# A hybrid decoder step on one core: weights streamed by half chunks, biases within the parts, and 21 dots moved between tiles

## The chip, the core and the metric

The kernel runs on one core of one Trainium2 chip, in one launch, all in float32. A core has five engines, each with an instruction queue of its own: PE (TensorE, matmul), DVE (VectorE), ACT (ScalarE), POOL (GpSimd) and SP (SyncE, which here issues loads and stores); 16 DMA engines serve them all. The engines meet at semaphores. The metric is the device time of one launch in microseconds (us), lower is better. TensorE's clock has two levels, 1.2 and 2.4 GHz; the profile shows the share that was granted.

## The reference, cut to what matters

512 prompt tokens and 8 x 4 sample tokens go through one layer of width 1024.

```python
mod = silu(c) @ ada_w + ada_b                 # 12 pieces of 512 columns, one row per sequence
sh1, sc1, gt1, sh2, sc2, gt2 = split(mod, 6)
h = rmsnorm(x, g_mix) * (1 + sc1) + sh1
z = h @ w_in                                  # 1024 x 3336
hm = mlstm(q, k, v, gates, C, n, m)           # 4 heads of 128, matrix memory C
oa = swa(sq, sk, sv, sinks, window=128)       # 4 heads, 2 of keys and values
yc = cb * short_conv(cc * ch, conv_w)
x = x + gt1 * (concat(hm, oa, yc) @ w_out)
h = rmsnorm(x, g_ffn) * (1 + sc2) + sh2
q = h @ wq                                    # 8 heads, two half keys each
idx, g = top 16 of the sums of the two top 16 # of 128 x 128 experts
act = gelu(einsum('thkd,td->thk', u_tab[idx], h))
x = x + gt2 * einsum('thk,thkd->td', g * act, v_tab[idx])
y = rmsnorm(x, final_g)
```

Each token needs 128 rows of `u_tab` (a dot product each) and 128 rows of `v_tab` (a weighted sum), 4 KB a row.

## The kernel before, in words

**Two parts.** The mixer comes first, up to a barrier at about 681 us; then the experts' part, which gathers rows of the two tables and works on them.

**The mixer's tiles.** The prompt is four tiles of 128 tokens, the sample is one tile of 32. Ahead of tile 0 stands a first stage that makes four of the twelve modulation rows; the tails of tiles 0 and 1 make the other eight. A modulation row takes three steps on PE: `ada_part` (L1344) multiplies the eight 128-row pieces of a chunk of `ada_w` in four column groups of 32, ACT copies the part, and `ada_row` (L1351, L1352) or, for one row spread over 128 partitions, `ada_rows` (L1358, L1359) folds the four groups with one matmul and adds the bias with a second one, the pick. DVE copies the row (L1231) and SP stores it (L961). A tile goes through its seven chunks of `w_in` (`chunk`, L615; 392, 512, 512, 512, 384, 512 and 512 columns in the order gates, q, k, v, sv|cb, cc|ch, o), with the mLSTM, the attention and the convolution between them, then `w_out` (L696) and the residual (L888 to L892). The first four transposed pieces of the normed rows are copied by ACT, the others by DVE (L791, hT).

**The stream.** SP loads the chunks of `ada_w`, `w_in` and pieces of `peer_wq` in a fixed order through a ring of three slots of 2 MB (`w_stream`, class `Stream`, load at L257). Chunk k waits until chunk k-3 is used up; a `wq` piece of 1 MB takes a slot too. PE waits for a whole chunk (`landed`).

**The first tile's experts, ahead of time.** From tile 1 on the mixer also routes tile 0's tokens. From tile 2 on GpSimd gathers their 128 rows of `u_tab` per token (L346), one row for each of 128 tokens at a time, into a ring of eight buffers in `low_rows`; DVE takes the dot product with the tile's rows (L333) and so frees the buffer. Where the dots stand is a table, `DOTS_IN`: gaps B to J, R, A and Z of each tile's code on DVE, C to Z of the sample's. The rows lie in SBUF for tiles 2 and 3; for the sample DVE copies them to PSUM three times (`row_to`, L339).

**The sample's tile.** It also loads the key and value caches and, last, the state C (2 MB into the stream's slots, L1543); PE transposes C in eight steps (L1734), and DVE and ACT copy the odd and even ones out (L1650, L1593). DVE makes Km, keys masked by sequence (L1670), for PE's update of C (L1762 to L1776; DVE's L1690 adds it up).

**The seam.** After the barrier GpSimd makes five constants (L1917 to L1924), then begins to gather `v_tab` rows (L1946); SP loads what the experts need, `subkeys` among it, which PE transposes first (L2442).

Of the kernel before, what the change touches and what calls it, by code (L numbers as in the profile page):

```python
# [106 lines left out]
class ConstantBuffers:  # L107

    def __init__(self, nc, ctx, space):  # L110
# [5 lines left out]
        self.pool_ready = sem("const_pool")  # L116
# [32 lines left out]
def constants_pool(nc, pool, K, C):  # L149
# [52 lines left out]
    fill(K["bias"][:, :, :], [[0, AH], [-1, 2 * P]], ALU.is_ge, NEG, P, 1).then_inc(C.pool_ready, 1)  # L202

class Stream:

    def __init__(self, X, s, s2):
# [18 lines left out]
        self.adas = [c for kind, c in self.order if kind == "ada"]  # L227

    def where(self, kind, i):
        k = self.order.index((kind, i))  # L230
        return k, k % RING

    def landed(self, pe, kind, i):

        k, slot = self.where(kind, i)
        pe.wait_ge(self.X.stream_in[slot], 16 * (k // RING + 1))
        return slot
# [12 lines left out]
    def load(self, sp, I, kind, i):  # L250

        k, slot = self.where(kind, i)
        if k >= RING:
            self.consumed(sp, k - RING)
        a, b = (i * 512, i * 512 + 512) if kind == "ada" else (i * 256, i * 256 + 256) if kind == "wq" else CHUNKS[i]
        src = I["ada_w" if kind == "ada" else "peer_wq" if kind == "wq" else "w_in"][0].rearrange("(kc p) n -> p kc n", p=P)
        sp.dma_start(self.X.wr[:, slot, :, 0:b - a], src[:, :, a:b]).then_inc(self.X.stream_in[slot], 16)  # L257

class Modulation:  # L260

    def __init__(self, space):
# [6 lines left out]
        self.pick_all = space.take(12, 4 * P, "p (c r) -> p c r", r=P)  # L270
# [6 lines left out]
DOTS_IN = {(2, "C"): 3, (2, "D"): 2, (2, "E"): 8, (2, "F"): 4, (2, "H"): 3, (2, "I"): 2, (2, "J"): 6, (2, "R"): 2, (2, "A"): 3,  # L277
# [9 lines left out]
AHEAD_SIGNALS = ("a_sub_in a_rows_in a_sq a_sq_ready a_h_ready piece_full piece_out keys_done a_routed a_used a_step").split()  # L287

class Ahead:  # L290
# [64 lines left out]
    def act_squares(self, act):  # L355
# [7 lines left out]
    def norm(self, dve, chain):
# [4 lines left out]
        dve.wait_ge(s["a_sq_ready"], 1)  # L368
# [4 lines left out]
    def pe_point(self, pe, t, w, e):  # L373
# [107 lines left out]
class Mixer:  # L481

    def __init__(self, nc, ctx):
# [3 lines left out]
        def ps(name, shape):  # L488
# [3 lines left out]
        self.stream_in = [nc.alloc_semaphore(f"mix_stream_in{i}") for i in range(RING)]  # L492
# [60 lines left out]
ADA_SIGNALS = ("ada_c_in c_sgm c_silu ct_ps ct_ready picks bias_in gain_in part_full part_out row_full row_ready row_out0 row_out1 "  # L553
               "rows_full").split()

class Tile:
# [49 lines left out]
    def chunk(self, pe, i):  # L607
# [5 lines left out]
        slot = X.stream.landed(pe, self.kind, i)  # L613
        for kc in range(KC):
# [171 lines left out]
    def dve_front(self, dve, chain, K, behind_rows=None):  # L786
# [44 lines left out]
        if self.kind == "sample":  # L831
            dve.wait_ge(s["m_in"], 16)
# [1707 lines left out]
```

## Time and profile before

| | us |
|---|---|
| median of 3 runs | 1984.42 (1981.6 to 1985.84) |
| the profiled execution | 1981.32 |
| its span | 1979.5 |
| PE busy | 1577.7 (80%) |
| DVE busy | 1212.3 (61%) |
| POOL busy | 1096.7 (55%) |
| ACT busy | 466.6 (24%) |

Busy shares are means over stretches that differ: in the experts' part the DMA engines are always busy, in the mixer the engine that ends a stretch last changes. So the busy times are read by stretch, and the waits at the end of each. In a row of a timeline the first number is the start, the second the duration of the group; `[2.88 <-DMA ...]` is the idle time just before it and what ended it.

### The profile page before, as it was taken

How to read it: one execution, taken by the hardware profiler on the slowest of the kernel's cores; microseconds unless marked ns; L12 is line 12 of the kernel's file. 1: busy time of each engine (PE TensorE's matmuls, PEld its weight loads, DVE VectorE, ACT ScalarE, POOL GpSimd, SP SyncE). 2: the span in 40 equal slices, each digit the busy share in tenths (PEclk: the TensorE clock that was granted, in tenths of full speed). 3: DMA queues.
4: the chain of work that ended last, by engine and by line, in shares of the span. 5: the costliest groups of instructions: out<-in, count | busy, mean ns of one | idle time of the engine just before them, and what ended most of it. 6: DMA issues, size and time to landing. Idle time of an engine off the chain costs nothing.

```text
span 1979.5 us, 17753 instructions
## 1 busy us (share of the span) xinstructions
PE 1577.7 (80%) x5461; PEld 734.4 (37%) x5461; DVE 1212.3 (61%) x3132; ACT 466.6 (24%) x1212; POOL 1096.7 (55%) x1168
## 2 busy tenths in 40 slices
PE   6989987788767568768888888888888788899933
PEld 1534544545236113223333343333433344344400
DVE  2223266886866602116767776877667679889973
ACT  1131311312102121212222222231222222323321
POOL 3000033443342245777777777777767677677774
PEclk8989998988875689998999999999999899999966
DMA  9696669798896599999999999999999999999996
GB/s 330 239 365 215 225 232 363 262 355 311 248 393 211 188 413 385 411 405 389 408 419 420 420 419 419 419 419 420 419 402 420 393 412 416 391 414 417 417 353 259
DMA packets 237565, 713.42 MB, mean 360 GB/s; under 512 B 23102, under 2 KB 49056, under 8 KB 237457
## 3 DMA queue, kind: packets, MB, share of 16 engines
q0 software_dynamic: 156672, 570.49, 72.8%
q1 hardware_dynamic: 80488, 140.73, 20.1%
q10 hardware_dynamic: 312, 1.07, 0.2%
q8 instruction: 45, 0.74, 0.1%
q14 instruction: 48, 0.39, 0.0%
HBM read 704.42 MB, written 8.25 MB: 360 GB/s over the span
## 4 chain that ended last, share of the span: by engine, by line
DMA 20%; PE 16%; POOL 13%; DVE 10%; issue 5%; ACT 2%; POOLq 0%; ACTq 0%; DVEq 0%
DMA v_rows<-in_peer_v_dram,expert_idx_ring 12%; PE ps_y L2373 9%; POOL u_rows L1932 6%; DMA v_rows<-in_peer_v_dram,tile_idx 5%; DVE u_rows L2152 5%; POOL v_rows L1938 5%; PE ps_r L2347 4%; POOL v_rows L1946 2%; DMA u_rows<-in_peer_u_dram,expert_idx_ring 2%; PE ps_y L2401 2%; ACT wt_diag L2043 1%; DVE key_scores_w L2163 0%; DVE top_i L2165 0%; DMA v_rows<-in_peer_v_dram,sample_idx 0%; DVE top L2164 0%
## 5 line engine op out<-in xcount | busy, mean ns | idle before, releaser
L2373 PE MATMUL ps_y<-v_rows,wt_diag 128*128 128x512 f32 x1536 | 731.6, 609 | 135.4 <-DMA v_rows<-in_peer_v_dram,expert_idx_ring 111.3
L2152 DVE CUSTOM_DVE_ANT_0 u_rows<-u_rows,ps_y 128x1024 f32<-128x1024 f32 x360 | 422.8, 1218 | 109.4 <-DMA u_rows<-in_peer_u_dram,expert_idx_ring 108.5
L2373 PEld LDWEIGHTS ps_y<-v_rows,wt_diag 128*128 128x128 f32 x1536 | 272.8, 191 | 533.9 <-issue 475.2
L1932 POOL DMA_INDIRECT u_rows<-in_peer_u_dram,expert_idx_ring x384 | 366.2, 954 | 137.4 <-issue 100.9
L1938 POOL DMA_INDIRECT v_rows<-in_peer_v_dram,expert_idx_ring x384 | 365.5, 952 | 118.7 <-issue 98.9
L615 PE MATMUL ps_z<-w_stream,hT 128*128 128x512 f32 (+5 forms) x560 | 252.1, 609 | 45.6 <-DMA w_stream<-in_w_in_dram 24.4
L346 POOL DMA_INDIRECT low_rows<-in_peer_u_dram,tile_idx x128 | 140.2, 1095 | 232.0 <-DVE tile_dots L333 169.2
L2401 PE MATMUL ps_y<-v_rows,wt_diag 64*64 64x512 f32 x1024 | 134.2, 643 | 58.5 <-DMA v_rows<-in_peer_v_dram,tile_idx 52.0
L615 PEld LDWEIGHTS ps_z<-w_stream,hT 128*128 128x128 f32 (+1 forms) x560 | 103.3, 189 | 173.4 <-issue 139.0
L1946 POOL DMA_INDIRECT v_rows<-in_peer_v_dram,tile_idx x128 | 123.4, 964 | 72.2 <-PE ps_y L2401 45.2
L2162 DVE MAX8 top<-key_scores 128x8 f32<-128x128 f32 x64 | 18.2, 285 | 172.2 <-ACT key_scores L2023 172.2
L2347 PE MATMUL ps_r<-wq,hT_next 128*128 128x256 f32 x512 | 116.9, 382 | 5.0 <-ACT hT_next L2013 5.0
L2043 ACT ACTIVATE wt_diag<-ident,wts 128x128 f32<-128x128 f32 x384 | 117.4, 388 | 14.2 <-DVE wts L2158 14.2
L2039 ACT ACTIVATE act_val<-dots 128x8 f32<-128x8 f32 x48 | 10.0, 209 | 456.1 <-DVE dots L2152 456.1
L2347 PEld LDWEIGHTS ps_r<-wq,hT_next 128*128 128x128 f32 x512 | 97.3, 191 | 32.9 <-issue 15.7
L899 POOL TENSOR_TENSOR z_cc_ch<-z_cc_ch 128x256 f32<-128x256 f32 (+1 forms) x5 | 3.6, 727 | 186.3 <-DVE z_cc_ch L840 186.3
L2401 PEld LDWEIGHTS ps_y<-v_rows,wt_diag 64*64 64x64 f32 x1024 | 39.6, 139 | 147.4 <-issue 117.2
L2152 DVE CUSTOM_DVE_ANT_0 u_rows<-u_rows,h_cur 128x1024 f32<-128x1024 f32 x24 | 28.9, 1233 | 91.1 <-DMA u_rows<-in_peer_u_dram,expert_idx_ring 91.1
L333 DVE CUSTOM_DVE_ANT_0 low_rows<-low_rows,tile_rows 128x1024 f32<-128x1024 f32 x63 | 75.6, 1250 | 7.1 <-DMA low_rows<-in_peer_u_dram,tile_idx 7.1
L696 PE MATMUL ps_z<-w_out,qT_kT 128*128 128x512 f32 (+1 forms) x160 | 74.0, 622 | 4.7 <-DVE low_rows L1231 4.7
L333 DVE CUSTOM_DVE_ANT_0 low_rows<-low_rows,ps_n 128x1024 f32<-128x1024 f32 x47 | 56.0, 1216 | 12.6 <-DMA low_rows<-in_peer_u_dram,tile_idx 12.2
L2386 PE MATMUL ps_y<-v_rows,wt_diag 128*32 128x512 f32 x96 | 21.4, 1039 | 46.9 <-DMA v_rows<-in_peer_v_dram,sample_idx 46.9
(444 smaller groups left out, 1722.0 us busy)
## 6 DMA issues: line engine op xcount, KB each, us to landing
w_stream<-in_w_in_dram SPq DMA_DIRECT2D x25, 2048.0 KB, 13.0
w_stream<-in_ada_w_dram SPq DMA_DIRECT2D x12, 2048.0 KB, 12.9
w_stream<-in_peer_wq_dram SPq DMA_DIRECT2D x8, 1024.0 KB, 9.5
wq<-in_peer_wq_dram SPq DMA_DIRECT2D x4, 2048.0 KB, 42.5
w_stream<-in_w_in_dram SPq DMA_DIRECT2D x5, 1568.0 KB, 8.5
w_stream<-in_w_in_dram SPq DMA_DIRECT2D x5, 1536.0 KB, 16.2
u_rows<-in_peer_u_dram,expert_idx_ring POOLq DMA_INDIRECT x384, 10.5
v_rows<-in_peer_v_dram,expert_idx_ring POOLq DMA_INDIRECT x384, 10.8
```

Source lines behind the costliest of these rows:

```text
L333: self.nc.vector.tensor_tensor_reduce(self.rows[:, k % NB, :], self.rows[:, k % NB, :], self.row, 1.0, 0.0, ALU.mult, ALU.add, self.keep[" ...
L346: self.nc.gpsimd.indirect_dma_start(self.rows[:, k % NB, :], None, U, bass.IndirectOffsetOnAxis(self.keep["idx0"][:, k:k + 1], 0)).then_in ...
L615: mm = self.nc.tensor.matmul(X.ps_z[i % 2][0:n, 0:b - a], X.hT[:, kc, 0:n], X.wr[:, slot, kc, 0:b - a], start=(kc == 0), stop=(kc == KC - 1))
L696: mm = nc.tensor.matmul(X.ps_z[c][0:n, :], X.mixT[:, kc, 0:n], X.w_out[:, kc, c * 512:(c + 1) * 512], start=(i == 0), stop=(i == KC - 1))
L1932: g.indirect_dma_start(u_rows[:, j, :], None, U, bass.IndirectOffsetOnAxis(where[:, j:j + 1], 0))\
L1938: g.indirect_dma_start(v_rows[:, j, :], None, V, bass.IndirectOffsetOnAxis(where[:, j:j + 1], 0))\
L1946: g.indirect_dma_start(v_rows[:, j, :], None, V, bass.IndirectOffsetOnAxis(idx0[:, k:k + 1], 0))\
L2043: a(diag[:, par, j, :], K["ident"][:, :], ACT.Copy, scale=wts[:, par, j:j + 1])\
L2152: v.tensor_tensor_reduce(u_rows[:, j, :], u_rows[:, j, :], row[:, :], 1.0, 0.0, ALU.mult, ALU.add, dots[:, par, j:j + 1]).then_inc(s["u_us ...
L2347: mm = nc.tensor.matmul(ps_r[:, 0, 0:256], hT[:, kc, :], wq[:, kc, bass.ds(h * 256, 256)], start=(kc == 0), stop=(kc == KC - 1))
L2373: mm = nc.tensor.matmul(ps_y[:, c * 512:(c + 1) * 512], diag[:, par, j, :], v_rows[:, j, c * 512:(c + 1) * 512], start=(first and j == 0), ...
L2401: mm = nc.tensor.matmul(ps_q[b * HP:(b + 1) * HP, half, c * 512:(c + 1) * 512], diag[rows, i % 2, j + b, 0:HP], v_rows[rows, j + b, c * 51 ...
```

## The change

It has five parts. **Halves:** the ring has six half slots of 1 MB. A chunk of `ada_w` or `w_in` comes as two loads of four 128-row pieces each, with a semaphore for each half slot; PE begins when the first half is there, and a half's slot is loaded again when that half is used (`half_used`, or the chunk's own signal for the second). A `wq` piece takes one half slot. **Bias:** `ada_part` adds the bias with one pick in its first half, and the picks behind the folds are gone, `pick_all` with them. **Constants:** GpSimd makes the experts' five constants at the start of the mixer. **Dots:** 21 of the 128 move from the sample's gaps to those of tiles 2 (5) and 3 (16); the prompt tiles had 66 and now have 87, the sample 62 and now 41. **Sample:** ACT makes the three row copies, all eight copies of C's transposes and Km. A number of semaphores are merged.

```diff
 class Stream:
...
-    def consumed(self, sp, k):
-        kind, i = self.order[k]
-        if kind == "ada":
+        kind, i, half = self.parts[k]
+        if kind == "wq":
+            sp.wait_ge(self.s["piece_full"], PIECES.index(("q", i)) + 1)
+        elif half == 0:
+            sp.wait_ge(self.s["half_used"], self.firsts.index((kind, i)) + 1)
+        elif kind == "ada":
             sp.wait_ge(self.s["part_full"], self.adas.index(i) + 1)
...
-        if k >= RING:
-            self.consumed(sp, k - RING)
-        sp.dma_start(self.X.wr[:, slot, :, 0:b - a], src[:, :, a:b]).then_inc(self.X.stream_in[slot], 16)
+        for half in range(1 if kind == "wq" else 2):
+            k, slot = self.where(kind, i, half)
+            if k >= HALVES:
+                self.consumed(sp, k - HALVES)
...
+            sp.dma_start(dst, part).then_inc(self.X.stream_in[slot], 16)
...
-DOTS_IN = {(2, "C"): 3, (2, "D"): 2, (2, "E"): 8, (2, "F"): 4, (2, "H"): 3, (2, "I"): 2, (2, "J"): 6, (2, "R"): 2, (2, "A"): 3,
-           (3, "B"): 2, (3, "C"): 3, (3, "D"): 2, (3, "E"): 6, (3, "F"): 7, (3, "G"): 4, (3, "I"): 2, (3, "R"): 4, (3, "Z"): 3,
-           ("sample", "C"): 5, ("sample", "D"): 3, ("sample", "E"): 7, ("sample", "F"): 5, ("sample", "G"): 6,
-           ("sample", "K"): 4, ("sample", "L"): 4, ("sample", "N"): 14, ("sample", "O"): 12, ("sample", "Z"): 2}
+DOTS_IN = {(2, "C"): 3, (2, "D"): 2, (2, "E"): 8, (2, "F"): 6, (2, "H"): 3, (2, "I"): 3, (2, "J"): 6, (2, "R"): 3, (2, "A"): 4,
+           (3, "B"): 4, (3, "C"): 4, (3, "D"): 4, (3, "E"): 7, (3, "F"): 8, (3, "G"): 5, (3, "H"): 2, (3, "I"): 4, (3, "J"): 3,
+           (3, "R"): 5, (3, "Z"): 3,
+           ("sample", "C"): 3, ("sample", "D"): 2, ("sample", "E"): 5, ("sample", "F"): 3, ("sample", "G"): 4,
+           ("sample", "K"): 3, ("sample", "L"): 3, ("sample", "N"): 8, ("sample", "O"): 8, ("sample", "Z"): 2}
...
-        slot = X.stream.landed(pe, self.kind, i)
-        for kc in range(KC):
+        for half in range(2):
+            w = X.stream.landed(pe, self.kind, i, half)
+            for k in range(HC):
...
+            mm.then_inc(X.stream.s["half_used"] if half == 0 else self.s[f"zfull{i % 2}"], 1)
...
             def ada_part(c, bank):
...
+                for half in range(2):
+                    w = stream.landed(pe, "ada", c, half)
+                    for j in range(HC):
+                        mm = nc.tensor.matmul(bank[32 * j:32 * (j + 1), :], M.cT[:, half * HC + j, :], w[:, j, :],
+                                              start=(half == 0), stop=(half == 1), skip_group_check=True)
+                        if half == 0 and j == 0:
+                            mm = nc.tensor.matmul(bank[0:NC, :], M.pick[:, c, :], M.bias[:, :], start=False, stop=False,
+                                                  skip_group_check=True)
+                    mm.then_inc(s["half_used"] if half == 0 else s["part_full"], 1)
...
-                nc.tensor.matmul(bank[0:NC, :], M.fold[:, :], M.part[:, nth(c) % 2, :], start=True, stop=False)
-                nc.tensor.matmul(bank[0:NC, :], M.pick[:, c, :], M.bias[:, :], start=False, stop=True)\
+                nc.tensor.matmul(bank[0:NC, :], M.fold[:, :], M.part[:, nth(c) % 2, :], start=True, stop=True)\
                     .then_inc(s["row_full"], 1)
...
     def on_scalar(act):
...
+        act.wait_ge(before["state_ready"], NT)
+        X.ahead.row_to(act, X.ps_n01, s)
...
+        T.z_out(act, OZ)
+        X.ahead.row_to(act, X.ps_z01, s)
...
+        for b in range(B):
+            last = a(Km[:, :, b, :], X.kz[0:NS, :].rearrange("p (h k) -> p h k", h=MH), ACT.Copy, scale=K["same"][:, b:b + 1])
+        last.then_inc(s["km_ready"], 1)
...
-        for i in range(0, B, 2):
+        for i in range(B):
             act.wait_ge(s["ct_full"], i + 1)
-            a(CTs[:, 4 * i:4 * i + 4, :], X.ps_s[:, 0, :], ACT.Copy).then_inc(s["ct_even_out"], 1)
+            a(CTs[:, 4 * i:4 * i + 4, :], X.ps_s[:, i % 2, :], ACT.Copy).then_inc(s["ct_out"], 1)
...
     def on_vector(dve, left):
...
-        for h in range(MH):
-            last = v.tensor_tensor(Km[:, h], repeat_mid(X.kz[0:NS, h * DH:(h + 1) * DH], B), repeat_last(same, DH),
-                                   ALU.mult)
-        last.then_inc(s["km_ready"], 1)
```

How this moves instructions is shown at three places. The first is PE's first stage, the parts of the modulation and the rows made of them (`ps_n` holds parts, `ps_s` rows over 128 partitions, `ps_z` rows of nine). Before:

```order
L1344 MATMUL ps_n<-w_stream,low_rows 32x512 x16
L1358 MATMUL ps_s<-low_rows 128x512
L1359 MATMUL ps_s<-low_rows 128x512
L1351 MATMUL ps_z<-low_rows 9x512
L1352 MATMUL ps_z<-low_rows 9x512
```

After:

```order
L1368 MATMUL ps_n<-w_stream,low_rows 32x512
L1371 MATMUL ps_n<-low_rows 9x512
L1368 MATMUL ps_n<-w_stream,low_rows 32x512 x8
L1371 MATMUL ps_n<-low_rows 9x512
L1368 MATMUL ps_n<-w_stream,low_rows 32x512 x7
L1384 MATMUL ps_s<-low_rows 128x512
L1378 MATMUL ps_z<-low_rows 9x512
```

The pick (L1371) stands behind the first matmul of each part, and a row has one matmul where it had two.

The second is SP around the start of tile 2, from the store of tile 1's rows on, with the semaphores that each load waits for (`zfull`: a chunk of `w_in` is used, `piece_full`: a `wq` piece is). Before:

```order
L976 DMA x_rows<-swa_scores 128x1024 [waits mix_x1_ready]
L966 DMA xt<-in_x_prompt_dram 128x1024 [waits mix_h_ready]
L257 DMA w_stream<-in_w_in_dram 128x8x512 [waits mix_zfull0]
L257 DMA w_stream<-in_w_in_dram 128x8x512 [waits mix_piece_full]
L257 DMA w_stream<-in_peer_wq_dram 128x8x256 [waits mix_zfull1]
L257 DMA w_stream<-in_w_in_dram 128x8x384 [waits mix_zfull0]
```

After:

```order
L1003 DMA x_rows<-swa_scores 128x1024 [waits mix_x1_ready]
L993 DMA xt<-in_x_prompt_dram 128x1024 [waits mix_h_ready]
L275 DMA w_stream<-in_w_in_dram 128x4x512 [waits mix_piece_full]
L275 DMA w_stream<-in_w_in_dram 128x4x512 [waits mix_half_used]
L275 DMA w_stream<-in_w_in_dram 128x4x512 [waits mix_zfull0]
L275 DMA w_stream<-in_w_in_dram 128x4x512 [waits mix_piece_full]
L275 DMA w_stream<-in_peer_wq_dram 128x8x256 [waits mix_half_used]
L275 DMA w_stream<-in_w_in_dram 128x4x384 [waits mix_zfull1]
```

The first load of the tile waited for all of chunk 0 of this tile; now its first half waits for a `wq` piece of tile 1 and its second for half of chunk 0.

The third is DVE in the sample's tail, between the last value weights and the mLSTM's norm. Before:

```order
L868 TENSOR_TENSOR diag_w<-z_v,last_val 32x512
L1664 TENSOR_TENSOR scratch<-same,last_val 32x32
L1665 TENSOR_TENSOR scratch<-last_s,last_val 32x32
L1667 COPY scratch<-last_val 32x4
L1668 COPY scratch<-m_t 32x4
L1670 TENSOR_TENSOR w_stream<-z_k,same 32x1024 x4
L876 RECIPROCAL r<-r 32x4
```

After:

```order
L895 TENSOR_TENSOR diag_w<-z_v,last_val 32x512
L1693 TENSOR_TENSOR scratch<-same,last_val 32x32
L1694 TENSOR_TENSOR scratch<-last_s,last_val 32x32
L1696 COPY scratch<-last_val 32x4
L1697 COPY scratch<-m_t 32x4
L903 RECIPROCAL r<-r 32x4
```

The four products for Km are no longer on DVE; on ACT they stand as eight copies behind those of the keys' cache.

## Rows read from the trace of the kernel before

**Rows 1.** The page: span, then loads with count, KB each, median us to landing.

```profile
span 1979.5 us, 17753 instructions
...
w_stream<-in_w_in_dram SPq DMA_DIRECT2D x25, 2048.0 KB, 13.0
...
w_stream<-in_peer_wq_dram SPq DMA_DIRECT2D x8, 1024.0 KB, 9.5
```

**Rows 2.** Busy times by stretch; the first line names the columns.

```profile
core 0: us, PE busy (x) PEld busy (x) DVE busy (x) ACT busy (x) POOL busy (x), PEclk, DMA share, GB/s
0.00:43.00 43.00, 28.04 (x111) 7.36 (x112) 10.00 (x23) 9.13 (x13) 14.96 (x53) 0.96 0.99 361
...
275.00:340.00 65.00, 49.15 (x138) 26.99 (x137) 41.53 (x122) 9.38 (x19) 31.32 (x25) 0.87 1.03 386
340.00:400.00 60.00, 49.68 (x216) 32.57 (x215) 51.96 (x138) 16.16 (x44) 22.72 (x20) 0.92 0.75 258
400.00:475.00 75.00, 64.64 (x214) 36.77 (x212) 53.16 (x142) 12.86 (x31) 30.17 (x26) 0.90 0.98 368
475.00:515.00 40.00, 30.89 (x115) 18.66 (x114) 33.48 (x95) 10.87 (x28) 10.23 (x8) 0.77 0.76 172
515.00:600.00 85.00, 61.59 (x192) 23.45 (x190) 58.93 (x137) 10.32 (x25) 35.41 (x38) 0.80 0.98 365
...
640.00:660.00 20.00, 19.98 (x36) 7.48 (x37) 13.82 (x44) 0.00 (x0) 0.00 (x0) 0.50 0.09 28
...
720.00:1979.00 1259.00, 1005.37 (x3316) 439.33 (x3316) 826.37 (x2146) 323.11 (x871) 904.01 (x939) 0.95 1.01 403
```

**Rows 3.** Timeline of the first stage: start, duration, engine, line.

```profile
17.21 1.92 PE L1344 MATMUL ps_n<-w_stream,low_rows 128*32 128x512 f32 x16 [1.70 <-DMA w_stream<-in_ada_w_dram]
...
37.08 0.60 ACT L1158 ACTIVATE mod_shift<-ps_s 128x512 f32<-128x512 f32 x1 [3.42 <-PE ps_s L1359]
...
37.93 1.02 PE L1352 MATMUL ps_z<-low_rows 12*9 12x512 f32 x2
...
47.35 0.69 DVE L791 COPY hT<-ps_t 128x512 f32<-128x512 f32 x1 [2.88 <-DMA conv_taps<-in_conv_w_dram]
```

**Rows 4.** Timeline of DVE at the end of tile 0.

```profile
148.18 0.68 DVE L1231 COPY low_rows<-ps_z 9x512 f32<-9x512 f32 x1 [5.41 <-DMA mod_rows<-low_rows]
```

**Rows 5.** Waits of PE, 250 to 400, then 400 to 500: total us, times, longest.

```profile
PE ps_z L615 <- DMA w_stream<-in_w_in_dram: 13.2, 4, 6.8
...
PE ps_z L615 <- DMA w_stream<-in_w_in_dram: 10.4, 3, 6.4
```

**Rows 6.** Timelines at the ends of tile 2 (PE) and tile 3 (DVE).

```profile
396.12 4.26 PE L615 MATMUL ps_z<-w_stream,hT 128*128 128x392 f32 x6 [6.35 <-DVE hT L791]
...
481.63 0.42 DVE L1276 TENSOR_TENSOR h<-ps_s,swa_sum 128x256 f32<-128x256 f32 x1 [1.37 <-PE ps_s L1422]
...
488.02 0.69 DVE L1285 COPY qT_kT<-ps_t 128x512 f32<-128x512 f32 x1 [1.21 <-PE ps_t L604]
...
493.42 1.22 DVE L333 CUSTOM_DVE_ANT_0 low_rows<-low_rows,tile_rows 128x1024 f32<-128x1024 f32 x1
```

**Rows 7.** Waits of PE in the sample, 500 to 681.

```profile
PE ps_s L1734 <- DMA w_stream<-in_state_mlstm_C_dram: 10.5, 1, 10.5
...
PE ps_s L646 <- DVE diag_w L822: 6.4, 1, 6.4
PE ps_t L604 <- DVE d_matrix L844: 6.3, 1, 6.3
...
PE ps_m L1762 <- DVE w_stream L1670: 2.2, 1, 2.2
```

**Rows 8.** Timeline of the sample's tail.

```profile
656.87 15.69 PE L696 MATMUL ps_z<-w_out,qT_kT 128*32 128x512 f32 x32
...
674.00 0.67 DVE L888 TENSOR_TENSOR z_q<-ps_z,mod_gate 32x512 f32<-32x512 f32 x1
```

**Rows 9.** Timeline of PE behind the barrier.

```profile
693.26 0.69 PE L2442 MATMUL ps_r<-ident,subkeys 128*128 128x128 f32 x2 [20.69 <-DMA subkeys<-in_peer_subkeys_dram]
```

More of the change, by code:

```diff
@@ L201, in constants_pool @@
     pool.wait_ge(C.cleared, AH + 3)
-    fill(K["bias"][:, :, :], [[0, AH], [-1, 2 * P]], ALU.is_ge, NEG, P, 1).then_inc(C.pool_ready, 1)
+    fill(K["bias"][:, :, :], [[0, AH], [-1, 2 * P]], ALU.is_ge, NEG, P, 1).then_inc(C.cleared, 1)
+    g.tensor_copy(K["iota_f"][:, :], K["iota16"][:, :])
+    g.memset(K["eps2"][:, :], EPS)
+    g.memset(K["gelu_warm"][:, :], 0.0)
+    g.tensor_tensor(K["half_ident"][:, :], K["ident"][:, 0:HP], K["ident"][:, HP:P], ALU.add)
+    g.memset(K["fold"][:, :], 0.0).then_inc(C.cleared, 1)
+    pool.wait_ge(C.cleared, AH + 5)
+    for i in range(QS):
+        fill(K["fold"][:, :], [[-1, NS]], ALU.not_equal, 1.0, -i * NS, 1).then_inc(C.cleared, 1)
+        pool.wait_ge(C.cleared, AH + 6 + i)
 class Stream:
@@ L227, in __init__, with where, landed @@
         self.adas = [c for kind, c in self.order if kind == "ada"]
[L229 to L237, printed above, removed]
-    def consumed(self, sp, k):
-        kind, i = self.order[k]
-        if kind == "ada":
+        self.parts = [(kind, c, half) for kind, c in self.order for half in range(1 if kind == "wq" else 2)]
+        self.firsts = [(kind, c) for kind, c in self.order if kind != "wq"]
+    def where(self, kind, i, half):
+        k = self.parts.index((kind, i, half))
+        return k, k % HALVES
+    def landed(self, pe, kind, i, half=0):
+        k, slot = self.where(kind, i, half)
+        pe.wait_ge(self.X.stream_in[slot], 16 * (k // HALVES + 1))
+        return self.X.wh[:, slot]
+    def consumed(self, sp, k):
+        kind, i, half = self.parts[k]
[4 more added lines that the diff above has]
+        elif kind == "ada":
             sp.wait_ge(self.s["part_full"], self.adas.index(i) + 1)
-        elif kind == "wq":
-            sp.wait_ge(self.s["piece_full"], PIECES.index(("q", i)) + 1)
         else:
@@ L393, in pe_point @@
         elif kind[0] == "q":
-            slot = X.stream.landed(pe, "wq", kind[1])
+            w = X.stream.landed(pe, "wq", kind[1]).rearrange("p a (two n) -> p (a two) n", two=2)
             for kc in range(KC):
-                last = nc.tensor.matmul(ps, self.hT[:, kc, :], X.wr[:, slot, kc, 0:256], start=(kc == 0), stop=(kc == KC - 1))
+                last = nc.tensor.matmul(ps, self.hT[:, kc, :], w[:, kc, :], start=(kc == 0), stop=(kc == KC - 1))
         elif kind[0] == "qT":
@@ L491, in __init__ @@
         self.wr = sb("w_stream", [P, RING, KC, 512])
-        self.stream_in = [nc.alloc_semaphore(f"mix_stream_in{i}") for i in range(RING)]
+        self.wh = self.wr[:, :, :, :].rearrange("p r (half k) n -> p (r half) k n", half=2)
+        self.stream_in = [nc.alloc_semaphore(f"mix_stream_in{i}") for i in range(HALVES)]
         self.low = sb("low_rows", [P, NB * D])
@@ L1357, in ada_rows @@
                 pe.wait_ge(s["part_out"], nth(c) + 1)
-                nc.tensor.matmul(bank, M.fold_all[:, :], M.part[:, nth(c) % 2, :], start=True, stop=False)
-                nc.tensor.matmul(bank, M.pick_all[:, c, :], M.bias[:, :], start=False, stop=True)\
+                nc.tensor.matmul(bank, M.fold_all[:, :], M.part[:, nth(c) % 2, :], start=True, stop=True)\
                     .then_inc(s["rows_full"], 1)
@@ L1599, in on_scalar @@
             .then_inc(s["oa_ready"], 1)
+        act.wait_ge(s["n_ready"], 1)
+        X.ahead.row_to(act, X.ps_n01, s)
     def on_vector(dve, left):
@@ L1606, in behind_rows @@
         def behind_rows(eng):
-            eng.wait_ge(before["piece_out"], len(PIECES))
-            X.ahead.row_to(chain, X.ps_n01)
+            X.ahead.row_in(eng, X.ps_n01, s, 1)
             left(eng)
```

115 lines of the change are left out of this document (48 added, 67 removed).

## The prediction, made before the changed kernel ran

> **What bounds the kernel now.** I read the page first, then the busy times of each engine by stretch, then PE's waits in each tile, then single instructions around the places that the change touches. The profiled execution took 1981.3 us, its span is 1979.5 us [rows 1]; the median of the runs shown is 1984.4, so 3.1 us is added to whatever the sum gives. The program has two parts. The experts' part, from 681 us, has the DMA engines busy all the time, at 403 GB/s [rows 2]; the change takes nothing from what it moves. So the change can win only in the mixer, the first 681 us, and at the seam between the parts. There the bound changes from stretch to stretch, and the reader should see in [rows 2] where the DMA share is near 1 and where it isn't: it is 1.03 in 275 to 340 and 0.98 in 400 to 475 and 515 to 600 (weights and gathers), 0.75 and 0.76 in 340 to 400 and 475 to 515 (DVE's work ends the tile there), and 0.09 in 640 to 660 (PE alone, at a granted clock of 0.50, the lower level of 1.2 GHz).
>
> Two prices are used throughout. A dot of the first tile costs DVE 1.15 us (the row is 1.22 long, the next starts 1.15 after it) [rows 6]. It also brings a gather of 128 rows of 4 KB, 0.52 MB: 0.52 / 0.386 = 1.36 us of all DMA engines in tile 2, 0.52 / 0.368 = 1.42 in tile 3, 0.52 / 0.365 = 1.44 in the sample's stretch [rows 2]. Moving a dot from the sample to a prompt tile is nothing saved; it pays only where the one stretch is full and the other has a hole.
>
> **First stage, -2.8 us.** Each modulation row before is a matmul that folds the part and a matmul that picks the bias; PE needs 0.95 to 1.05 us for each (1.02 in the row, start to start 0.95) [rows 3]. PE works without a gap from the second part at 17.21 to the last pick, so eight picks out of its row shorten it. With its part in halves the last row's part has only its second half, about 1 of 1.92 us [rows 3], behind its data. I put `mod_shift`, which sits at 37.08 behind the last fold and pick [rows 3], 4.9 us earlier. But the copy of hT on DVE at 47.35 waits 2.88 for `conv_taps`, a small load at the end of SP's queue, behind the first weights [rows 3]. The DMA engines are at 0.99 up to 43 [rows 2], and the bytes ahead of the small loads don't change. So only about 2.8 of the 4.9 reaches PE; ends -1 (the small loads don't move but for their issue) and -5 (all of it).
>
> **Tiles 0 and 1, -3.5 us.** At the end of tile 0 PE waits for the last row copy, which has waited 5.41 us for the store of an earlier row [rows 4]. Six rows lose a pick (0.95 each, most of it hidden behind the stores), and their weights may be used by halves: -2.5, between 0 and -5. Tile 1 has two rows: -1, between 0 and -2.
>
> **Tile 2 up to its last weights, -9 us.** PE waits 13.2 us for four loads of `w_in` between 250 and 400, the longest 6.8 [rows 5]. Three things bear on it. PE starts on the first half: at 386 GB/s the second 1 MB takes 2.7 us or more beside gathers, and half a chunk is 3.5 us of PE, so each wait shrinks by at most some 3.5. A `wq` piece takes one half slot in place of a whole one, so the loads of chunk 2 and half of chunk 3 go out about 4 to 6 us earlier, into a stretch where the DMA engines still have room. Against it, gap F gets two dots, 2 x 1.36 = 2.7 us more DMA. Taken chunk by chunk the four waits can lose 0.8 + 3.5 + 3.5 + 0.8 = 8.6 by the halves alone, some 3 more by the earlier loads: -9 after the gathers; ends -4 (halves of two waits only) and -13 (all of it).
>
> **End of tile 2, +3.5 us.** DVE is busy for 52 of the 60 us from 340 to 400 [rows 2], and PE stands 6.35 us at 396.12 for DVE's hT [rows 6]. Three more dots (I, R, A) lie there: 3 x 1.15 = +3.5. Nothing hides them; the DMA share of 0.75 takes their gathers.
>
> **Tile 3 up to 475, +4 us.** Eight more dots (B 2, C 1, D 2, E 1, F 1, G 1) bring 8 x 1.42 = 11.4 us of DMA to a stretch with share 0.98 [rows 2]. DVE has room for them (53 busy of 75 us). Against that the three waits for weights, 10.4 us, longest 6.4 [rows 5], lose up to 0.3 + 3.5 + 3.5 = 7.3 by the halves. Net +4. Ends: -6 (halves give all, earlier loads fill the holes ahead of 410, the gathers stay under the ring of eight) and +11.4 (gathers paid in full, halves nothing).
>
> **End of tile 3, +6.6 us.** Eight more dots (H 2, I 2, J 3, R 1) x 1.15 = 9.2 us on a DVE that sets the end: 33.5 of 40 us busy [rows 2]. H and I stand ahead of the wait of 1.37 at L1276 or just behind it, J ahead of the 1.21 at L1285 [rows 6]; they take up these 2.6: 9.2 - 2.6 = +6.6. Ends +3 (`h` is ready earlier because the tile started earlier, so PE's results are waited for less) and +9.2. Their gathers (8 x 0.52 MB) fall in 475 to 515, where the DMA engines have 24% free [rows 2], and cost nothing.
>
> **Sample up to the state C, -14 us.** This is the place that pays. From 515 to 600 the DMA engines are at 0.98 and C, the last thing PE waits for (10.5 us), lands when their queue is empty [rows 2, 7]. Dots C, D, E, F, G, K, L go from 34 to 23, and gathers run eight ahead of dots both before and after, so 11 gathers fewer stand ahead of C: 11 x 1.44 = 15.8 us. PE allows it: of its waits there 6.4 (diag), 6.3 (d_matrix) and 10.5 (C) are to go [rows 7], and the first two are waits for DVE, which loses the same dots. I take -14; ends -6 (PE's wait for d_matrix alone) and -23 (all three waits). Copying the tile's rows moves from DVE to ACT, which idles here; it hides behind the residual.
>
> **Tail of the sample, -3.6 us.** The four products with `same` (Km) leave DVE: PE's wait of 2.2 for them goes [rows 7]. Then L1776 and `w_out` follow without a gap, so PE ends at 656.87 + 15.69 - 2.2 = 670.4 [rows 8]. The residual's first step now stands at 674.00 behind twelve dots and the row copy [rows 8]; with four dots and the copy gone it could start at 674.0 - 4 x 1.15 - 1.2 = 668.2, so PE binds: 674.0 - 670.4 = -3.6. Ends -2 and -5. Cover of the edits: ACT makes Km while it waits for the caches, and all eight copies of C's transposes, 0.6 us each beside 0.95 us of PE transposes each; should ACT be late, up to 1 us comes back.
>
> **Seam, -1.2 us.** GpSimd makes the experts' constants from the end of the mixer on, and they hold its first gather back by 2.5 us, from 680.6 to 683.1. But PE's first instruction there waits 20.69 us for `subkeys` [rows 9], on the same DMA engines. Earlier gathers move 2.5 us of traffic forward, and part of it goes before `subkeys`: -1.2, ends -2.5 and +2.
>
> **Sum.** -2.8 - 3.5 - 9 + 3.5 + 4 + 6.6 - 14 - 3.6 - 1.2 = -20.0. From 1981.3 that is 1961.3, on the scale of the median 1964.4.
>
> **Rivals.** (a) Slower: the gathers delay the weights in tiles 2 and 3. Loads of weights and gathers lie in different queues and share the engines; if the halves come in between gathers, they land together and PE gains nothing by the first. Then tile 2 costs +2.7 in place of -9, tile 3 +11.4 in place of +4, its end +9.2: the sum is -20.0 + 11.7 + 7.4 + 2.6 = +1.7, and with the low ends of tiles 0 and 1 and of the sample (+3.5, and +8) it is +13: 1997. It decides for slower than before once the weights in tiles 2 and 3 together lose 20 us against the forecast. For it speaks the share of 1.03; against it the idle DMA ahead of 275 and in 340 to 400. Chance 0.09. (b) More: C lands so early that PE isn't idle long before it. Then the clock needn't fall to 0.50 in the stretch up to 660 [rows 2], PE's 20 us there and its transposes halve until DVE binds, some -10, and with the high ends of tile 2 and the sample (-4, -5) the sum is -39: 1945. Against it: 23 us of PE's waits stand ahead of C [rows 7]. Chance 0.14. (c) The halves and the pick within the part don't do as they say: the pick stands alone between the column groups, so that a part takes 1.92 + 0.95 = 2.9 us, and two loads of 1 MB are slower than one of 2 MB (9.5 us from issue to landing for 1.0 MB, 13.0 for 2.0, both among others [rows 1]). Without a gain in the first stage, in tiles 0 and 1, and with a third of it in tile 2: -20.0 + 2.8 + 3.5 + 6 = -7.7, 1977. The stretches at 1.03 run on loads of 2 MB and can't show how halves do. Chance 0.17. The rule on drained tiling modes, named above, speaks for the first half of this rival. The forecast keeps 0.60, with an own range of 1953 to 1974.
>
> **Chances.** A measurement of this kernel can tell some 0.2%, 4 us, from no change. Faster takes the forecast, (b) and most of (c): 0.83. Same, 1980.4 to 1988.4, takes the rest of (c), the lower half of (a) and the forecast's far tail: 0.09. Slower 0.08. The range reaches from (b), 1945, over (c) to 1982, a little beyond it; what lies outside is (a) and the far side of (b).
>
> **What would show it.** hT's copy in the first stage at 44 to 45 rather than 47.35; PE's waits for `w_in` in tile 2 from 13.2 to 5 or less and in tile 3 below 8; tile 3's residual about as late, relative to that tile's start, as 10 us more; PE's d_matrix and diag waits in the sample gone, C landing some 14 us sooner after the tile's start; no wait at Km; the residual right behind `w_out`. Wrong it is if PE's waits for weights in tiles 2 and 3 stay at their 23.6 us, if C's landing moves by less than 6, or if a part of the modulation takes 3 us.

## The result: slower by 0.6%, for a reason that none of the terms held

The changed kernel takes 1998.7 us (median of 9 runs, 1992.9 to 2004.0), the kernel before on the same chips 1985.8 (1976.4 to 1997.0): a ratio of 1.0059, interval 1.0036 to 1.0082. Forecast were 1964.4, with 1945 to 1982 as the range. The sign was wrong, and the time lies near the rival of the slower side (1997), but not by its mechanism.

Where the time went is plain once the program is cut at the points that the prediction used. These are starts of PE's instructions (of DVE's for the residual) in the two profiled executions (us); the step is how far the gap between before and after moves from one point to the next.

| point on PE | before | after | after - before | step | forecast |
|---|---|---|---|---|---|
| tile 0 begins | 48.10 | 49.16 | +1.1 | +1.1 | -2.8 |
| tile 2 begins | 269.01 | 269.34 | +0.3 | -0.7 | -3.5 |
| tile 2's last chunk | 345.17 | 342.84 | -2.3 | -2.7 | -9 |
| tile 3 begins | 396.12 | 397.54 | +1.4 | +3.8 | +3.5 |
| tile 3's last chunk | 467.60 | 472.94 | +5.3 | +3.9 | +4 |
| sample begins | 511.12 | 522.25 | +11.1 | +5.8 | +6.6 |
| C is transposed | 606.16 | 603.46 | -2.7 | -13.8 | -14 |
| residual (DVE) | 674.00 | 666.58 | -7.4 | -4.7 | -3.6 |
| `subkeys` behind the barrier | 693.26 | 686.70 | -6.6 | +0.9 | -1.2 |
| end of the span | 1979.5 | 2000.1 | +20.6 | +27.2 | 0 |

Up to `subkeys` the changed kernel is 6.6 us ahead. Then the experts' part, where the change moves no work but GpSimd's five constants, takes 27 us longer. This is the page of the changed kernel (loads with count, KB each and median us to landing, as in [rows 1]):

```profile
span 2000.1 us, 17791 instructions
...
w_stream<-in_w_in_dram SPq DMA_DIRECT2D x50, 1024.0 KB, 11.4
...
w_stream<-in_peer_wq_dram SPq DMA_DIRECT2D x8, 1024.0 KB, 12.3
```

And its busy times by stretch, columns as in [rows 2]:

```profile
275.00:340.00 65.00, 53.09 (x162) 30.06 (x161) 46.41 (x132) 9.68 (x20) 34.47 (x28) 0.89 1.04 391
340.00:400.00 60.00, 46.12 (x197) 29.79 (x197) 51.87 (x135) 15.87 (x44) 26.83 (x22) 0.90 0.74 263
400.00:475.00 75.00, 61.19 (x199) 34.89 (x198) 60.79 (x147) 10.37 (x21) 41.33 (x34) 0.87 1.03 393
475.00:515.00 40.00, 31.15 (x124) 17.74 (x122) 34.88 (x91) 14.37 (x39) 21.38 (x16) 0.87 0.96 286
515.00:600.00 85.00, 65.13 (x201) 23.91 (x199) 53.32 (x148) 16.25 (x35) 25.12 (x27) 0.82 0.98 339
...
1000.00:1200.00 200.00, 168.34 (x430) 75.19 (x430) 138.31 (x343) 51.28 (x136) 146.88 (x157) 0.99 1.03 409
...
720.00:2000.00 1280.00, 1006.09 (x3292) 438.96 (x3284) 827.58 (x2146) 321.26 (x863) 899.52 (x936) 0.96 1.00 394
```

The same stretch of the experts' part in the kernel before:

```profile
1000.00:1200.00 200.00, 170.65 (x437) 76.46 (x437) 142.31 (x362) 51.27 (x136) 149.94 (x160) 0.99 1.03 419
```

With the DMA engines at the same share, 1.03, they move 409 GB/s in place of 419. That is 2.4% of 1286 us, or 31 us; 27 are seen. The gathers are the same. What differs is where their targets lie: the five constants are now allocated with the mixer's, ahead of everything, and no longer among the experts' tiles. In the program's list of allocations `v_rows` and `u_rows`, into which the gathers write, start at 161024 and 128256 bytes in each partition before (multiples of 256) and at 161216 and 128448 after (192 past one). The mixer's stream (`w_stream`) and its gather ring (`low_rows`) move by exactly 512 bytes, from 224 past a multiple of 256 to 224 past one.

In the first stage the pick splits the part (rows of the third of four parts, then DVE; x2 is one matmul, which PE makes in two passes):

```profile
30.73 1.02 PE L1368 MATMUL ps_n<-w_stream,low_rows 128*32 128x512 f32 x2
31.68 1.02 PE L1371 MATMUL ps_n<-low_rows 12*9 12x512 f32 x2
32.63 1.92 PE L1368 MATMUL ps_n<-w_stream,low_rows 128*32 128x512 f32 x14
...
48.41 0.69 DVE L818 COPY hT<-ps_t 128x512 f32<-128x512 f32 x1 [3.37 <-DMA conv_taps<-in_conv_w_dram]
```

The first matmul runs alone, the pick alone, the other seven in four groups: 3.8 us for a part that took 1.92 in [rows 3].

PE's waits for weights, 250 to 400 and then 400 to 520, answer [rows 5]:

```profile
PE ps_z L642 <- DMA w_stream<-in_w_in_dram: 6.5, 3, 2.3
PE ps_n L420 <- DMA w_stream<-in_peer_wq_dram: 5.4, 1, 5.4
...
PE ps_n L420 <- DMA w_stream<-in_peer_wq_dram: 7.7, 1, 7.7
PE ps_z L642 <- DMA w_stream<-in_w_in_dram: 6.1, 3, 2.7
```

For `w_in` they fall from 13.2 and 10.4 to 6.5 and 6.1. Much of that comes back as a wait for a `wq` piece: 5.4 in place of 2.6 in tile 2, and 7.7 in place of none in tile 3, where eight more gathers run beside the loads.

### The profile page after: what moved, and what is told of

The parts are those of the page before. It is cut to its first block, busy times and chain, and to the rows that moved or that the text cites. A ratio compares the mean times of both kernels' runs of the same rounds, so it can differ in the third digit from the quotient of the medians.

```text
span 2000.1 us, 17791 instructions
## 1 busy us (share of the span) xinstructions
PE 1588.8 (79%) x5453; PEld 731.1 (37%) x5453; DVE 1200.1 (60%) x3121; ACT 477.5 (24%) x1230; POOL 1103.1 (55%) x1166
## 4 chain that ended last, share of the span: by engine, by line
DMA 22%; PE 16%; POOL 13%; DVE 8%; issue 5%; ACT 2%; SPq 0%; POOLq 0%; ACTq 0%; DVEq 0%
DMA v_rows<-in_peer_v_dram,expert_idx_ring 15%; PE ps_y L2383 9%; POOL u_rows L1944 6%; POOL v_rows L1950 5%; DMA v_rows<-in_peer_v_dram,tile_idx 5%; DVE u_rows L2163 4%; PE ps_r L2357 4%; POOL v_rows L1958 2%; PE ps_y L2411 2%; ACT wt_diag L2055 1%; DMA subkeys<-in_peer_subkeys_dram 1%; DMA u_rows<-in_peer_u_dram,expert_idx_ring 1%; DVE key_scores_w L2174 1%; DVE top_i L2176 1%; DMA v_rows<-in_peer_v_dram,sample_idx 0%
## 5 line engine op out<-in xcount | busy, mean ns | idle before, releaser
L370 POOL DMA_INDIRECT low_rows<-in_peer_u_dram,tile_idx x128 | 150.0, 1172 | 210.0 <-DVE tile_dots L351 139.3
L351 DVE CUSTOM_DVE_ANT_0 low_rows<-low_rows,tile_rows 128x1024 f32<-128x1024 f32 x84 | 100.5, 1250 | 4.5 <-DMA low_rows<-in_peer_u_dram,tile_idx 4.5
L2064 ACT ACTIVATE wt_diag<-half_ident,tile_dots 128x64 f32<-128x64 f32 x128 | 32.2, 334 | 86.3 <-PE ps_y L2411 85.8
## 6 DMA issues: line engine op xcount, KB each, us to landing
w_stream<-in_w_in_dram SPq DMA_DIRECT2D x50, 1024.0 KB, 11.4
```

The lines of the kernel that those rows point to most:

```text
L351: self.nc.vector.tensor_tensor_reduce(self.rows[:, k % NB, :], self.rows[:, k % NB, :], self.row, 1.0, 0.0, ALU.mult, ALU.add, self.keep[" ...
L370: self.nc.gpsimd.indirect_dma_start(self.rows[:, k % NB, :], None, U, bass.IndirectOffsetOnAxis(self.keep["idx0"][:, k:k + 1], 0)).then_in ...
```

## The experiments

Two readings stood against each other: the address of the gathers' targets, or something at the seam that upsets the traffic behind it. The first four runs tell them apart.

**The changed kernel, buffers back on a multiple of 256.**

```diff
+        pad = sb("pad", [P, 16])
         half_ident, y2 = K["half_ident"], sb("y_halves", [P, 2, D])
```

> The changed kernel with 64 unused bytes a partition ahead of the experts' buffers, so that the gathers' targets (u_rows, v_rows) start at a multiple of 256 bytes again, as in the kernel before; nothing else. Theory (where the gathers land in SBUF sets their rate): the plateau in the experts' part goes back from 409 to 419 GB/s, that part gets some 27 us shorter, the time is about 1972. Rival (the earlier constants and gathers, or the half loads, upset the order of traffic at the seam, and the experts' part pays for it throughout): the pad changes nothing, 409 GB/s and about 1998.

Measured: 1971.8 us (1968.0 to 1976.0), ratio to before 0.9915 (0.9884 to 0.9945). Sixty-four unused bytes are worth 27 us in the medians; from `subkeys` to the end its profile has 1289.4 us where the changed kernel has 1313.4. The row of its experts' part:

```profile
1000.00:1200.00 200.00, 171.49 (x438) 76.74 (x438) 142.42 (x362) 50.21 (x137) 149.94 (x160) 0.99 1.03 419
```

**The kernel before, buffers 192 past a multiple of 256.**

```diff
-        half_ident, y2 = sb("half_ident", [P, HP]), sb("y_halves", [P, 2, D])
+        half_ident, pad, y2 = sb("half_ident", [P, HP]), sb("pad", [P, 48]), sb("y_halves", [P, 2, D])
```

> The kernel before with 192 unused bytes a partition ahead of the experts' buffers, so that u_rows and v_rows start 192 bytes past a multiple of 256, as in the changed kernel; nothing else. Theory of the address: the plateau falls from 419 to 409 GB/s, the time rises by some 27 us to about 2012. Rival of the seam: no change, about 1985.

Measured: 2007.5 us, ratio 1.0093 (1.0059 to 1.0128); somewhat less than was expected, 20 us rather than 27, but the rate is the one of the changed kernel, and from `subkeys` to the end its profile has 1313.8 us, as the changed kernel (1313.4), against 1286.2 before:

```profile
1000.00:1200.00 200.00, 167.71 (x426) 74.50 (x425) 142.35 (x360) 51.02 (x135) 146.38 (x157) 0.99 1.03 409
```

The two runs settle it: the address sets the rate, with the change and without it. The seam falls as a cause. A pad moves every tile behind it and not the two gather targets alone, but in this stretch the DMA engines write nothing else. This is what they move from 1000 to 1200 in the kernel before (queue with packets, MB and share; loads with count and median us to landing):

```profile
q0 software_dynamic: 23010, 83.79, 102.5%
...
v_rows<-in_peer_v_dram,expert_idx_ring POOLq DMA_INDIRECT x80, 9.0
u_rows<-in_peer_u_dram,expert_idx_ring POOLq DMA_INDIRECT x80, 8.9
```

Over all thirteen profiles the two groups lie apart: from `subkeys` to the end the nine with aligned targets take 1285.7 to 1291.2 us, the four with targets off a multiple 1313.4 to 1318.2.

**The kernel before, the mixer's stream moved to a multiple of 256.**

```diff
+        self.pad = sb("pad_mix", [P, 8])
         self.wr = sb("w_stream", [P, RING, KC, 512])
```

> The kernel before with 32 unused bytes a partition ahead of the mixer's weight stream, so that the stream and the mixer's gather ring start at a multiple of 256 bytes (before: 224 past one); the experts' part is as before. If the address sets the rate of weights as well as of gathers, the 300 us of the mixer with full DMA engines gain 2 to 5%: 6 to 12 us less, about 1976, with the experts' plateau at 419. If the address matters only to the gathers of the experts' part: within 3 us of before.

Measured: 1971.0 us, ratio 0.9905 (0.9868 to 0.9941). In 400 to 475, where [rows 2] have 368 GB/s at share 0.98, it has

```profile
400.00:475.00 75.00, 68.14 (x260) 42.35 (x258) 57.83 (x160) 19.71 (x49) 31.15 (x28) 0.93 1.01 390
```

Weights and gathers run together there, and the pad moves the targets of both. From 10 to 30, before any gather, the loads of weights are alone; before, then with the pad:

```profile
10.00:30.00 20.00, 16.41 (x76) 3.57 (x80) 2.74 (x4) 1.79 (x3) 6.07 (x9) 1.00 1.05 387
```

```profile
10.00:30.00 20.00, 16.45 (x64) 3.26 (x64) 2.06 (x3) 1.79 (x3) 6.42 (x11) 1.00 1.05 407
```

So the weights' loads gain by themselves, 5% at the same share; the kernel before had this loss in its mixer all along.

**The changed kernel with both pads.**

> The changed kernel with both pads (64 bytes ahead of the experts' buffers, 32 ahead of the mixer's stream). Theory of the address: the gains of the two pads add, about 1964, the experts' plateau at 419 GB/s. Rival of the seam: about 1998, or 1990 if only the mixer's pad acts.

Measured: 1959.5 us, ratio 0.9859 (0.9815 to 0.9904). The gains add, some 5 us better than was expected; 400 to 475 now moves 412 GB/s, where the kernel with the 64 bytes alone moves 396 at the same share:

```profile
400.00:475.00 75.00, 61.43 (x229) 36.26 (x227) 61.85 (x157) 17.21 (x41) 39.38 (x33) 0.90 1.04 412
```

**Two other offsets**, timed once each; the edit is that of the second run with 8 and with 32 columns of padding.

> The kernel before with 32 unused bytes ahead of the experts' buffers (gathers land 32 past a multiple of 256). If each gathered row pays for the bytes between the last multiple of 256 and its start, 32 bytes of 4096 cost a sixth of what 192 cost: a plateau of 417 GB/s. If a row that starts off a multiple of 256 pays one more piece whatever the offset: 409 as at 192.

> The kernel before with 128 unused bytes ahead of the experts' buffers (gathers land 128 past a multiple of 256). Paying by bytes: two thirds of the loss at 192, 412 GB/s. Paying by piece: 409. If a multiple of 128 is enough: 419.

Measured: 2015.1 and 2014.9 us, and the same rate at 32 and at 128 past a multiple of 256:

```profile
1000.00:1200.00 200.00, 164.71 (x415) 71.39 (x414) 140.57 (x358) 48.49 (x127) 146.35 (x156) 1.00 1.03 409
```

```profile
1000.00:1200.00 200.00, 166.65 (x417) 72.50 (x416) 140.46 (x357) 48.36 (x126) 145.97 (x156) 0.99 1.03 409
```

At the three offsets tried, 32, 128 and 192, a start off the multiple costs the same rate; paying by bytes falls.

The other runs take the mixer's terms apart.

**Dots as before, with the 64 bytes only**: the changed kernel with the old table `DOTS_IN`.

> The changed kernel with the 64 bytes ahead of the experts' buffers (mixer's stream left 224 past a multiple of 256) and the dots where they stood in the kernel before. It measures the move of 21 dots in the mixer as it was predicted, with a slow stream. The prediction's terms for the dots: +2.7, +3.5, +11.4, +6.6 in the prompt tiles against -14 and about -2 in the sample, +8 or so in all; measured in the profile of the changed kernel: +13 from tile 2 to the sample's start and -14 ahead of C. Theory (the move loses): 1965, some 7 less than with the pad alone (1972). Rival (it pays where DMA is slow): 1976 or more.

Measured: 1964.4 us, ratio 0.9879 (0.9849 to 0.9909), 7.3 less than with the moved dots (0.9915, 0.9884 to 0.9945; the intervals overlap). Here is the sample's first chunk in this kernel, then in the one with the moved dots and the same pad:

```profile
492.79 14.17 PE L641 MATMUL ps_z<-w_stream,hT 128*32 128x392 f32 x32 [6.24 <-DVE hT L817]
```

```profile
516.12 9.43 PE L642 MATMUL ps_z<-w_stream,hT 128*32 128x392 f32 x19 [7.08 <-DVE hT L818]
```

The move delays the sample by 23.3 us and wins back 15.8 of them ahead of C (587.4 against 595.0). The profile says that it loses, and the time leans the same way.

**Dots as before, with both pads.**

> The changed kernel with both pads and the dots where they stood in the kernel before (66 in the prompt tiles, 62 in the sample). Theory (moving 21 dots costs 3.5 + 6.6 us of DVE at the ends of tiles 2 and 3 and some DMA in tile 3, and saves 14 us ahead of C and some 2 in the tail): without the move the sample starts some 8 to 11 us earlier and C is transposed some 4 to 8 later; the time is about 1965, 6 more than 1959. Rival (in a mixer with aligned buffers the DMA engines are no longer what the sample waits for, and the move of dots costs more than it brings): about 1955.

Measured: 1954.1 us (1950.7 to 1957.0), ratio 0.9835 (0.979 to 0.988). The point that I had put first, that the move pays by 6, fell; the rival's 1955 fits. Its reason, that aligned buffers take the DMA engines out of the way, doesn't: with the slow stream above the move loses as much. Against 1959.5 the intervals overlap again, but both pairs point one way, and the profile agrees with the run above: `subkeys` is reached at 663.3 rather than 670.2.

**The pick behind the fourth matmul**, with both pads.

```diff
-                        if half == 0 and j == 0:
+                        if half == 0 and j == HC - 1:
```

> The changed kernel with both pads and the bias pick moved within the part: behind the fourth matmul of the first half, not behind the first. Theory (a pick of 12 rows runs alone and splits the four column groups: 1.0 us for the first matmul, 1.0 for the pick, 1.9 for the seven others): behind the fourth the part takes 0.96 + 0.95 + 0.96 = 2.9 us in place of 3.8, the four parts of the first stage give back some 3.6 us of PE, and the time falls by 1 to 4 from 1959 (as it stands beside the two pads alone). Rival (the pick costs 0.95 wherever it stands, and the split costs nothing): parts stay at 3.8 us and the time at 1959.

Measured: 1959.1 us, ratio 0.9862 (0.9816 to 0.9908): no gain that could be told. The third part and PE's next wait:

```profile
20.39 1.42 PE L1369 MATMUL ps_n<-w_stream,low_rows 128*32 128x512 f32 x5
21.73 1.02 PE L1372 MATMUL ps_n<-low_rows 12*9 12x512 f32 x2
22.69 1.06 PE L1369 MATMUL ps_n<-w_stream,low_rows 128*32 128x512 f32 x8
...
45.87 2.98 PE L643 MATMUL ps_z<-w_stream,hT 128*128 128x392 f32 x4 [8.65 <-DVE hT L819]
```

The second half of a part is down to 1.06, and PE ends the first stage at 32.6, 2.7 us earlier than in the run with both pads (35.3). It then waits 8.65 us for DVE's hT, where that run waits 4.76, and tile 0 begins at 45.87 and 45.54: nothing is won. hT waits for the small loads. Where the pick stands costs PE's time as the theory has it, and not the kernel's.

**Whole chunks**: both pads, loads in halves, but PE waits for both halves of a chunk of `w_in`.

```diff
+        X.stream.landed(pe, self.kind, i, 1)
         for half in range(2):
             w = X.stream.landed(pe, self.kind, i, half)
```

> The changed kernel with both pads, but PE waits for both halves of a chunk of w_in before its first matmul; the loads stay in halves, with six half slots. It tells PE's early start from the deeper ring. Theory (early start is what halves give): PE's waits for w_in in tiles 2 and 3 rise by 2 to 3 us for each of five or six chunks, about 1970. Rival (a full DMA queue delivers at its own rate, and what PE gains at a first half it waits out at the second or at the next piece of wq): within 4 us of 1959.

Measured: 1968.3 us, ratio 0.9907 (0.9878 to 0.9935), 9 more than with the early start. Its waits ahead of a chunk (named "issue", since two semaphores follow each other), 250 to 400:

```profile
PE ps_z L644 <- issue: 11.3, 2, 5.8
...
PE ps_n L420 <- DMA w_stream<-in_peer_wq_dram: 2.2, 1, 2.2
```

With the early start the two are 5.0 and 6.1 there, so part of what PE gains at the first half is waited out at `wq`. Beginning on the first half is worth some 9 us by the medians and 5.6 by the profiles up to `subkeys` (675.8 against 670.2); the intervals overlap by a little (0.9878 to 0.9904), so the size is not settled.

**A version that beats both**: both pads, dots as before, the late pick, and the six small loads issued behind the third load of `ada_w`.

> Both pads, dots as before, the pick behind the fourth matmul of a part, and the six small loads (gate_b, mlstm_g, sinks, conv_taps) issued behind the third load of ada_w, not behind the row stores and the first weights of w_in. Theory (the first stage ends with those small loads, behind the weights in SP's queue, whatever PE needs): hT's copy on DVE follows its transposes at some 37 to 38 us, tile 0 starts 7 to 8 earlier than 45.9, and the time is about 1947. Rival (the first weights of w_in or the DMA engines set the start): tile 0 still starts at 44 or later, 1953.

Measured: 1948.4 us (1941.4 to 1951.2), ratio 0.9803 (0.9782 to 0.9824). Tile 0 starts at 43.0, 2.9 earlier and not 7 to 8. The next thing late is DVE itself: its last row copies wait for the store of an earlier row, then it makes tiles for the sample (`s_bias`) up to 42.3, and only then copies hT:

```profile
38.28 1.28 DVE L1256 COPY low_rows<-ps_z 9x512 f32<-9x512 f32 x2 [2.19 <-DMA mod_rows<-low_rows]
...
43.01 9.36 PE L642 MATMUL ps_z<-w_stream,hT 128*128 128x392 f32 x20 [4.34 <-DVE hT L818]
```

## Why the prediction was wrong

**The step that failed is the first one**: "the change takes nothing from what it moves", so "the change can win only in the mixer". The experts' part was given a term of zero because its work, order and bytes were the same. It is bound by the DMA engines for 1286 us, and moving five small constants to another place of the allocation changed the address of every buffer behind them. I had weighed what each instruction does and not where its tiles lie; the program's allocations show that shift in both kernels before any run. That it costs 2.4% of the rate, no row of before showed. With the rate of before (the 64 bytes) the changed kernel has a ratio of 0.9915: 17 us faster, 1967 on the scale of the forecast's 1984.4, well within the range. Put right by this alone, the forecast of 1964.4 would have been 3 off.

That is in part luck, since the terms beneath it err both ways. They can be read twice: the kernel with the 64 bytes has the same mixer at the same addresses, so its profile is a second one of these stretches. Its steps against before, at the points of the table above:

| point | tile 0 | tile 2 | its last chunk | tile 3 | its last chunk | sample | C | residual | `subkeys` | end |
|---|---|---|---|---|---|---|---|---|---|---|
| changed kernel | +1.1 | -0.7 | -2.7 | +3.8 | +3.9 | +5.8 | -13.8 | -4.7 | +0.9 | +27.2 |
| with 64 bytes | -0.5 | -2.0 | -6.7 | +3.6 | +4.1 | +6.5 | -16.2 | -2.6 | +0.8 | +3.1 |

Up to `subkeys` the second gains 13.0 us where the first gains 6.6, and 20 were forecast. Steps of the mixer differ by up to 4 us between two executions of the same code; the dots and the experts' part stand clear of that.

- **First stage, -2.8: +1.1 and -0.5.** The pick's price in the part, taken as 0.3, is 1.9 (3.8 against 1.92), more than rival (c) gave it, since the pick also cuts the first matmul off from the others. The rule of the Trainium skill that I named against it (page TensorEngine Tiling (Array Packing), section Key Properties), that changing the tiling mode drains TensorE, agrees with the trace, though no run separates this reason from another. But the late pick shows that even without this nothing reaches the end: the small loads are the floor, as the prediction said. Its reason was wrong. They don't wait for the bytes ahead of them: `conv_taps` lands 2.2 to 2.4 us after it is issued. It is issued late, because SP first waits for DVE's last copies of modulation rows and stores them. SP in the changed kernel:

```profile
41.70 0.89 SPq L988 DMA_DIRECT2D mod_rows<-low_rows  x2
...
45.18 1.46 SPq L1019 DMA_DIRECT2D conv_taps<-in_conv_w_dram  x3
```

- **Tile 2's weights, -9: -2.7 and -6.7.** PE's waits for `w_in` fell by 6.7 of 13.2, where the halves alone were to give 8.6. The `wq` wait, 2.6 before, rose to 5.4; I had no term for it. In the profile with the 64 bytes the two are 8.1 and 2.4, so their sum goes from 15.8 to 11.9 and 10.5, and how it divides changes from one execution to the next. Rival (a), that the two halves of a chunk land together, is refuted by the changed kernel's rows, where PE works on a first half and then waits for the second:

```profile
314.84 2.75 PE L642 MATMUL ps_z<-w_stream,hT 128*128 128x384 f32 x8
319.81 4.54 PE L642 MATMUL ps_z<-w_stream,hT 128*128 128x384 f32 x8 [2.22 <-DMA w_stream<-in_w_in_dram]
```

- **The dots.** Each size was right: +3.5, +4 and +6.6 were forecast in the prompt tiles and +3.8, +3.9 and +5.8 seen, -14 and -13.8 ahead of C, and the second profile agrees. What was wrong was the verdict in words, "the place that pays": inside tiles 2 and 3 the halves' gain and the dots' cost stood in one term. Taken apart from the same terms, the dots cost 2.7 + 3.5 + 11.4 + 6.6 = 24 and win 14 and some 2; the pair with the 64 bytes has 23.3 and 15.8, and 7.3 us in the time.
- **Tail, -3.6: -4.7 and -2.6**, right. The wait for Km is gone and the residual follows `w_out`, as these rows of the changed kernel show beside [rows 8]:

```profile
650.71 15.76 PE L723 MATMUL ps_z<-w_out,qT_kT 128*32 128x512 f32 x32
...
666.58 0.68 DVE L915 TENSOR_TENSOR z_q<-ps_z,mod_gate 32x512 f32<-32x512 f32 x1 [5.51 <-PE ps_z L723]
```

- **Seam, -1.2: +0.9 and +0.8.** The first gather starts 7.3 us behind the residual's begin and not 9.1, but `subkeys` still ends PE's wait, 20.23 against 20.69 [rows 9]:

```profile
686.70 0.69 PE L2452 MATMUL ps_r<-ident,subkeys 128*128 128x128 f32 x2 [20.23 <-DMA subkeys<-in_peer_subkeys_dram]
```

One sum of the prediction is off by itself: rival (b) takes -5 from the sample, but the far end named there, -23 in place of -14, gives -9, so that this rival's time would be 1941 and not 1945.

## What to carry to other kernels

When an edit adds, removes or moves a tile, compare the addresses of all the tiles behind it, first of those that DMA engines write in a stretch that they bound: here 64 bytes of padding are 27 us, and 32 more ahead of the weights are 12. Split a term that nets a gain against a cost before calling a part of the change good: the move of dots lost by its own numbers. And before shortening work ahead of a wait for several things, look which of them comes last and what holds it; here six small loads ended the first stage, and it was their place in SP's program, behind stores that wait for DVE, and not the bytes ahead of them.

## What the runs showed of the hardware

Rows of 4 KB that land in SBUF at a multiple of 256 bytes move at 419 GB/s with the 16 engines full, those that land 32, 128 or 192 bytes past one at 409, the same for all three. Weights in runs of 2 KB, alone from 10 to 30, move at 387 GB/s with their buffer 224 past a multiple (before) and at 407 on one (the same kernel with the stream moved by 32 bytes). In 400 to 475, weights and gathers together, the changed kernel moves 396 with the 64 bytes and 412 with both pads, at share 1.04. The loss is 2.4% for rows of 4 KB and 5% for runs of 2 KB. An estimate from these four rates, with 16 engines sharing them, is some 4 ns of one engine for each run that starts off a multiple, of either length.

The Trainium skill, page DMA: Bandwidth & Descriptors, section How a descriptor splits into AXI transactions, says that a descriptor not starting at a multiple of 256 bytes is fetched from the boundary below and pays for the bytes between. It speaks of reads, and the runs moved the place of writes. The direction agrees. The size doesn't: by that account 32 bytes would cost an estimated 1 beat in 128 and 192 bytes 6, and the runs show 2.4% for either. Why it is the same for these offsets is open.

A matmul of 12 rows between matmuls in four column groups runs alone, and so does the one that it cuts off from its group: 1.02 and 1.02 us in the rows above. Behind the fourth matmul it cuts none off: it takes its 1.02, and the second half of the part 1.06.
